# A hybrid decoder step on one core: other order of the last mixer iteration and of the first expert blocks

## What is computed

```python
h = rmsnorm(x) * (1 + sc_m) + sh_m
u = h @ w_in                      # conv_a | conv_b | q | k | v | g
y = concat[conv branch, retention branch] @ w_out
x = x + gt_m * y
h = rmsnorm(x) * (1 + sc_f) + sh_f
scores = sigmoid(h @ w_router)    # 64 experts: 4 of 8 groups kept, then 6 experts of a token
x = x + gt_f * (shared(h) + sum of the 6 experts' weight * expert(h))
y = rmsnorm(x, g_final)           # expert: (silu(h@w1) * (h@w3)) @ w2, hidden width 256
```

## Time and profile before

| | |
|---|---|
| median of 3 runs | 1592.87 us (1591.91 to 1594.37) |
| profiled execution, its time | 1594.62 us |
| its span in the profile | 1592.8 us |
| PE busy | 1439.1 us, 90% |
| DVE busy | 830.8 us, 52% |
| POOL busy | 493.3 us, 31% |
| HBM read, written | 323.10 MB, 62.13 MB |

### The profile page before, as it was taken

The page is one execution under the profiler, slowest core; times in us unless marked ns, Lnnn a source line. Parts: engine busy times, 40 slices in busy tenths (PEclk is TensorE's granted clock), DMA queues, the critical chain, the costliest instruction groups (busy, mean ns, idle before and its releaser), DMA issues.

```text
span 1592.8 us, 17516 instructions
## 1 busy us (share of the span) xinstructions
PE 1439.1 (90%) x5855; PEld 644.2 (40%) x5855; DVE 830.8 (52%) x2113; ACT 217.5 (14%) x369; POOL 493.3 (31%) x426
## 2 busy tenths in 40 slices
PE   4899999999999999998579999899999999999947
PEld 2344454555545454733233343233344333333313
DVE  1147778998988999733533332332333333323317
ACT  1111231312222131322000000000000000000003
POOL 0001010121211111311545454444545454545410
PEclk8899999999999999788789999999999999999978
DMA  9987211211120000512499999999999999999976
GB/s 333 328 317 262 95 43 66 82 40 70 40 82 27 32 29 28 192 39 78 145 331 320 371 367 373 366 362 370 367 372 367 371 370 348 340 373 366 367 211 244
DMA packets 93436, 369.69 MB, mean 232 GB/s; under 512 B 17741, under 2 KB 29425, under 8 KB 68207
## 3 DMA queue, kind: packets, MB, share of 16 engines
q1 hardware_dynamic: 69383, 304.29, 49.0%
q0 software_dynamic: 23968, 64.35, 16.3%
HBM read 323.10 MB, written 62.13 MB: 242 GB/s over the span
## 4 chain that ended last, share of the span: by engine, by line
DMA 44%; PE 25%; DVE 17%; issue 7%; SPq 4%; ACT 2%; POOL 1%; POOLq 0%; DVEq 0%; ACTq 0%
DMA acc_rows<-xr,kT 20%; DMA acc_rows<-W,kT 17%; PE U L649 9%; DVE cv L1249 7%; PE R L703 7%; DMA acc_rows<-W,shared_f 3%; PE U L851 2%; SPq L400 2%; DMA W<-in_w_ada 2%; PE U L828 1%; PE R L613 1%; PE U L805 1%; SPq L407 1%; DMA acc_rows<-xr,shared_f 1%; DMA x_t<-h_rows,q_r 1%
## 5 line engine op out<-in xcount | busy, mean ns | idle before, releaser
L649 PE MATMUL U<-W,hT 128*128 128x512 f32 x864 | 386.5, 602 | 1.2 <-issue 1.2
L1249 DVE SCALAR_TENSOR_TENSOR cv<-win,cw,cv 128x128 f32<-128x128 f32 x960 | 254.8, 343 | 1.4
L867 PE MATMUL R<-W,glu 128*32 128x512 f32 (+2 forms) x1024 | 240.9, 597 | 1.3 <-DVE glu L1537 1.3
L851 PE MATMUL U<-W,cat 128*128 128x512 f32 (+2 forms) x736 | 236.1, 608 | 5.5 <-issue 3.0
L649 PEld LDWEIGHTS U<-W,hT 128*128 128x128 f32 x864 | 162.9, 193 | 189.0 <-issue 189.0
L851 PE MATMUL U<-W,hT 128*32 128x512 f32 (+2 forms) x1312 | 237.2, 601 | 0.0
L1524 DVE STREAM_TRANSPOSE hT<-x_t 128x1024 f32<-128x1024 f32 x33 | 67.4, 2042 | 217.4 <-DMA x_t<-h_rows,q_r 215.6
L1524 DVE STREAM_TRANSPOSE cat<-W 128x1024 f32<-128x1024 f32 x33 | 67.2, 2037 | 214.2 <-DMA W<-h_rows,q_r 181.8
L867 PEld LDWEIGHTS R<-W,glu 128*32 128x32 f32 (+2 forms) x1024 | 84.1, 138 | 150.2 <-issue 148.8
L851 PEld LDWEIGHTS U<-W,cat 128*128 128x128 f32 (+2 forms) x736 | 93.2, 163 | 124.7 <-issue 121.1
L1718 POOL DMA_INDIRECT x_t<-h_rows,q_r x124 | 125.1, 1009 | 37.9 <-issue 37.9
(11 more groups left out here) (293 smaller groups left out, 1187.3 us busy)
## 6 DMA issues: line engine op xcount, KB each, us to landing
W<-in_w SPq DMA_DIRECT2D x192, 1024.0 KB, 17.5
W<-in_w_ada SPq DMA_DIRECT2D x24, 1024.0 KB, 9.3
W<-in_w_in SPq DMA_DIRECT2D x6, 2048.0 KB, 19.9
W<-acc_rows SPq DMA_DIRECT2D x16, 512.0 KB, 9.6
h_rows<-xr SPq DMA_DIRECT2D x9, 512.0 KB, 2.7
x_t<-in_x_prompt SPq DMA_DIRECT2D x8, 512.0 KB
W<-in_w_out SPq DMA_DIRECT2D x1, 4096.0 KB, 17.7
xr<-in_x_prompt SPq DMA_DIRECT2D x8, 512.0 KB
```

Source lines behind the costliest of these rows:

```text
L649: last = mm(U[BANK[g]][:, :], hT[:, k, :], w_in[:, k, 512 * g:512 * g + 512], start=k == 0, stop=k == KT - 1)
L851: last = mm(U[1][cols, :], xgT[z][:, k, cols], w13[:, :, k, :], start=k == 0, stop=k == KT - 1)
L867: last = mm(R[cols, 512 * half:512 * half + 512], hidT[:, f, cols], weights[:, at:at + 512], start=f == 0, stop=f == FT - 1)
L1249: ins = v.scalar_tensor_tensor(cv[:, c, :], win[:, c, w:w + P], cw[:, c, w:w + 1], cv[:, c, :], ALU.mult, ALU.add)
```

## The change

- `AHEAD` is 2 in place of 4: blocks 0 and 1 are shared, block 2 is the first routed unit, then shared and routed blocks take turns until block 15. The planner `even_order`, which uses AHEAD, gives another order of the groups on the line.
- The ring's slots are numbered in the order (0, 3, 1, 2), so that the first two don't lie on the samples' states; the samples' scaled k moves into `late`.
- SyncE: storing `new_ret_sample`, and waiting for it, moves from ahead of the first weight load to behind the loads of places 0 and 1.
- TensorE in the last mixer part: `mix_out(7)` is cut in halves with the samples' small sums and transposes between them; the samples' output product (`few_out`) is cut in parts, with `positions(6)`, the transposes of tile 7 and `router(7)` between them; state products 0 to 2 come after it, 3 and 4 after the first shared `up`, 5 to 7 around `rank_products`. The samples' router comes ahead of the first shared `up`. `positions(8)` follows that `up`; `spread_lists` comes ahead of block 1.
- DVE: `top_k(6)` goes ahead of `norm2(7)`, `place(6)` right behind it, `top_k(7)` is cut in two with `sample_residual` between; `place(7)`, `top_k(8)`, `place(8)` and the ranking follow with no block work among them. Blocks 1 and 2 come after the list's numbers and not between them.
- ACT: `score(7)` ahead of the state updates, which are spread among later steps.
- GpSimd: only gathers 0 and 1 come ahead of the lists; scatters 0 and 1 come after `slot_ready`, behind `gather(2)` and `gather(3)`.

```diff
-AHEAD = 4
+AHEAD = 2
-        ring = [W[:, WE * (r + 1):WE * (r + 2)] for r in range(RING)] + [shw]
+        ring = [W[:, WE * (r + 1):WE * (r + 2)] for r in (0, 3, 1, 2)] + [shw]
-        k_s = k_d[0:NS, :]
+        k_s = late[0:NS, 0, 1024:1536]
@@ SyncE
-            sp.wait_ge(state_upd, 2 * H)
-            for b in range(NS):
-                sp.dma_start(out["new_ret_sample"][0, b].rearrange("h d e -> d h e"),
-                             S0[:, b // 2, b % 2, :, :]).then_inc(newret_out, 16)
-            sp.wait_ge(newret_out, 16 * (NS + 1))
-            for s in range(NE):
+            for s in range(2):
+                load_in_line(s)
+            sp.wait_ge(state_upd, 2 * H)
+            for b in range(NS):
+                sp.dma_start(out["new_ret_sample"][0, b].rearrange("h d e -> d h e"),
+                             S0[:, b // 2, b % 2, :, :]).then_inc(newret_out, 16)
+            sp.wait_ge(newret_out, 16 * (NS + 1))
+            for s in range(2, NE):
                 load_in_line(s)
@@ TensorE
-            mix_out(TP - 1)
+            mix_half(TP - 1, 0)
             few_sum(sq, sum2_done)
             few_rows(o_t[:, :, :].rearrange("p h e -> p (h e)"), R24, ret_posed)
+            mix_half(TP - 1, 1).then_inc(wout_done, 1)
+            few_out(0, 0, KT)
+            positions(TP - 2, pick, NT)
             rows2_trans(TP - 1, hT_ready, NT)
-            state_product(0)
-            state_product(1)
-            router(TP - 1, TP)
-            state_product(2)
-            state_product(3)
-            positions(TP - 2, pick, NT)
-            up(0, shw_all, 0)
+            few_out(1, 0, KT // 2)
+            router(TP - 1, TP)
+            few_out(1, KT // 2, KT).then_inc(wout_done, 1)
+            for n in range(3):
+                state_product(n)
+            positions(TP - 1, pick, NT)
...
-            for n in range(H, 2 * H):
-                state_product(n)
...
-            hidden_trans(0)
-            up(1, shw_all, 1)
-            pe.wait_ge(state_upd, 2 * H)
-            positions(TP - 1, pick, NT)
-            down(0, shw_all)
-            positions(TP, pick_s[:, :], NT)
-            hidden_trans(1)
-            rank_products()
+            up(0, shw_all, 0)
+            positions(TP, pick_s[:, :], NT)
+            for n in range(3, 5):
+                state_product(n)
+            rank_products()
+            state_product(5)
+            hidden_trans(0)
+            for n in range(6, 2 * H):
+                state_product(n)
+            spread_lists()
-            for x in range(2, NX):
+            for x in range(1, NX):
                 await_weights(x)
                 up(x, parts_of(x), x % 2)
+                if x == 1:
+                    pe.wait_ge(state_upd, 2 * H)
                 down(x - 1, parts_of(x - 1))
                 hidden_trans(x)
-                if x == 2:
-                    spread_lists()
@@ VectorE
             residual(TP - 1)
+            top_k(TP - 2)
             norm2(TP - 1)
-            top_k(TP - 2)
+            place(TP - 2, pick, NT)
+            groups_kept(TP - 1)
             sample_residual()
-            place(TP - 2, pick, NT)
+            experts_kept(TP - 1)
             sample_norm2()
-            top_k(TP - 1)
-            blk_hid(0)
-            blk_hidT(0)
-            xpose(1)
             place(TP - 1, pick, NT)
...
-            block(1)
...
-            block(2)
+            blk_hid(0)
+            xpose(1)
+            blk_hidT(0)
...
+            block(1)
+            block(2)
             block(3)
@@ GpSimd
             ret_out(TP)
+            fill_list(TP - 2)
             gather(1)
-            fill_list(TP - 2)
             fill_list(TP - 1)
-            gather(2)
             fill_list(TP, NS)
-            gather(3)
...
-            scatter(0)
-            scatter(1)
             pool.wait_ge(slot_ready, 2)
-            gather(4)
-            for x in range(2, NX):
+            gather(2)
+            for x in range(NX):
                 if x + 3 < NX:
                     gather(x + 3)
                 scatter(x)
```

More of the change, by code:

```diff
@@ L696, in positions, with mix_half, mix_out @@
                 mm(cnt_m, mean_w[:, :], chosen, start=True, stop=True).then_inc(pos_done, 1)
-            def mix_out(m):
+            def mix_half(m, n):
                 pe.wait_ge(catA_part, 4 * (m + 1))
                 pe.wait_ge(catB_ready, m + 1)
-                for n in range(2):
-                    for k in range(KT):
-                        last = mm(R[:, 512 * n:512 * n + 512], cat[:, k, :], w_out[:, k, 512 * n:512 * n + 512],
-                                  start=k == 0, stop=k == KT - 1)
-                last.then_inc(wout_done, 1)
+                for k in range(KT):
+                    last = mm(R[:, 512 * n:512 * n + 512], cat[:, k, :], w_out[:, k, 512 * n:512 * n + 512],
+                              start=k == 0, stop=k == KT - 1)
+                return last
+            def mix_out(m):
+                mix_half(m, 0)
+                mix_half(m, 1).then_inc(wout_done, 1)
             def body(i, front=True, tail=True, route=True, nxt=True, place=True):
@@ L822, in _, with few_out @@
             few_rows(o_t[:, :, :].rearrange("p h e -> p (h e)"), R24, ret_posed)
+            mix_half(TP - 1, 1).then_inc(wout_done, 1)
+            def few_out(n, first, last):
+                for k in range(first, last):
+                    ins = mm(U[n][0:NS, :], cat_s[:, k, :], w_out[:, k, 512 * n:512 * n + 512], start=k == 0, stop=k == KT - 1)
+                return ins
             pe.wait_ge(catA_part, 4 * NT)
@@ L825, in _ @@
             pe.wait_ge(k_rot, NT)
-            for n in range(2):
-                for k in range(KT):
-                    last = mm(U[n][0:NS, :], cat_s[:, k, :], w_out[:, k, 512 * n:512 * n + 512], start=k == 0, stop=k == KT - 1)
-            last.then_inc(wout_done, 1)
+            few_out(0, 0, KT)
+            positions(TP - 2, pick, NT)
             pe.wait_ge(sret_ready, 1)
             rows2_trans(TP - 1, hT_ready, NT)
+            few_out(1, 0, KT // 2)
+            pe.wait_ge(dest_ready, TP - 1)
+            router(TP - 1, TP)
+            few_out(1, KT // 2, KT).then_inc(wout_done, 1)
             pe.wait_ge(vmask_ready, 1)
-            state_product(0)
-            state_product(1)
-            router(TP - 1, TP)
-            state_product(2)
-            state_product(3)
-            pe.wait_ge(score_ready, TP)
-            positions(TP - 2, pick, NT)
+            for n in range(3):
+                state_product(n)
             def tiles_of(parts):
@@ L1142, in _ @@
             nc.scalar.activation(std2[0:NS, :], ssq2[0:NS, :], ACT.Sqrt, scale=1.0 / D, bias=eps_c[0:NS, 0:1]).then_inc(norm2_std, 1)
+            state_update(1)
+            state_update(2)
             act.wait_ge(h2_posed, NT)
             nc.scalar.activation(h2T[:, :, 0:NS], Xk[:, :, 0:NS], ACT.Copy).then_inc(h2T_ready, 1)
-            for n in range(H, 2 * H):
-                state_update(n)
             act.wait_ge(ret_ready, NT)
@@ L1151, in _ @@
             blk_silu(0)
+            for n in range(3, 2 * H):
+                state_update(n)
             for x in range(1, NX):
@@ L1275, in top_k, with groups_kept @@
             def top_k(m):
+                groups_kept(m)
+                experts_kept(m)
+            def groups_kept(m):
                 dve.wait_ge(score_ready, m + 1)
```

14 lines of the change are left out of this document (7 added, 7 removed).

## The result

The changed kernel takes 1574.74 us (median of four runs, 1572.82 to 1576.92), the kernel before 1593.17 (four runs, 1591.91 to 1594.37) on the same chip: a ratio of 0.9885, interval [0.9868, 0.9902], 18.4 us less. The forecast was 1580 in a range of 1566 to 1590.

What follows compares the result with a forecast made beforehand. The prediction took the serial string of expert-stage scatters as the clock, with PE and DMA just behind. Start 17, step 3 and tail -7 gave 13 us off the 1592.87 median: 1580, range 1566 to 1590.

Steps and rivals of the forecast that it cites:

- start, at scatter 4: Start of the expert stage: earlier list numbers bring scatter 4 from 844.72 to 828, 17 us gained.
- step: Time between successive scatters in the expert stage: loads spread over 64 blocks instead of 62, 3 us gained in all.
- tail: Last blocks: up(64) waits for place 62's down part, 8 us and 2 for the clock, partly absorbed; 7 us lost.
- The numbers sooner: Reordered work on the list's numbers before the expert stage: line_ready at 743 instead of 779.88, some 37 us sooner.
- What is ahead of 692 us doesn't change: Work before tile 7's residual: the same 32 mix_out matmuls, cut by small ones, so times count from the same start.
- From `line_ready` to the first routed up: List writes, list gathers, spreading, then gather and transpose: from line_ready at 743 to the up at 780.
- The stores cost nothing: Moving 2 MB of state stores behind the first weight loads on SP's queue would cost no time; issuing takes 6 us.
- the cover of 20: Slack for weights of places 2 and 3: loaded until 780, wanted at 803, hiding the moved stores.
- the string is the clock of this stage: Expert stage: serial scatters, each waiting for the last to land, set the pace at 11.35 us a step.
- the 0.15: Sign of being wrong: the step between scatters moves by more than 0.15 us, which 64 blocks turn into 10 us.
- rival 1: Expert stage: bytes set the step, which gains 16 us; total gain 26 us, 1567 us; chance 0.18.
- the rule on queues: DMA engines take packets in turn from queues with work, so longer weight queues wouldn't lengthen scatters; step stays 11.35 us.

Runs made afterwards that it cites:

- late_place: Changed kernel, but the last token tile's numbers are again worked out behind shared block 0's up part; 1597.86 us, ratio 1.0028 to the kernel before.
- half: Changed kernel, but from place 4 on each expert's down-part load is cut to 64 KB, so results are wrong; 1543.07 us, ratio 0.9676 to the kernel before.
- split_tail2: Changed kernel with its last expert group moved to -3, place 0 loaded before the stores, place 1 after the lists land; 1567.95 us, ratio 0.9829 to before.
- hold: Changed kernel with the first weight load held back until both gathers of lists have landed; 1579.69 us, ratio 0.9921 to the kernel before.
- tables: Changed kernel, but odd blocks scatter to a second pair of tables, so no scatter waits for the one before; 1573.50 us, ratio 0.9864 to before.
- ahead4: Changed kernel with AHEAD back at 4, so blocks 0 to 3 are shared; 1577.21 us, ratio 0.9887 to the kernel before.
- early: Changed kernel with state products 3 to 6 ahead of positions(8), first shared up behind the ranking, stores before all loads; 1581.48 us, ratio 0.9929 to before.

## Why the prediction was right, and where it was not

The time came out 5.3 us below the forecast, inside the range and just under the forecast's own 1575 to 1585. Measured from the start of `mix_out(7)` (673.56 in the trace that the forecast counted on), term by term:

| term | forecast | measured |
|---|---|---|
| start, at scatter 4 | 17 | 12.6 |
| step | 3 | 8.4 |
| tail | -7 | -3.0 |
| sum | 13 | 18 |

Each of the three is 4 to 5 us off, one of them the other way. That the sum is only 5 off is in part luck: the start's 4.4 us too much covered most of the step's 5.4 too little.

- **The numbers sooner: right.** 743 was forecast and 740.9 is there; from `mix_out` that is 69.4 forecast and 70.8 measured (here the end of its row, as in the forecast). `late_place` shows that this moment carries the change. Two of its pieces went another way than told. Some of the products of the states came at the lower clock (the row at 742.55, where the granted clock is 0.50: 2.07 us for two matmuls that took 1.12 at 740.11, at 1.00), and so did a part of `few_out` (5.43 us for 8 matmuls at 700.98, 3.60 for 8 at 708.27). The first lay beside the path; the second, ahead of the router, took 1.3 us more than the 4.1 forecast; the granted clock from 700 to 706 is 0.61.
- **"What is ahead of 692 us doesn't change": not so.** PE's matmuls of `mix_out(7)` began 3.5 us sooner in this execution. As the medians don't show this as a gain, it belongs to the execution. It makes the absolute moments (778.60 for 780, 828.60 for 828) look sooner than they are: from `mix_out` scatter 4 was 4.1 us later than forecast, at 158.5 for 154.4, though `half`, with the same code up to there, was at 154.4.
- **From `line_ready` to the first routed up: right,** 37.9 us for 37; it was 35.6 to 37.1 in the others with this order, 33.8 in `split_tail2` with half the early weights, and 30.9 in `hold` with none beside the lists (all from the start of `line_ready`'s row). So the weights that are loaded early lengthen it by up to 7 us, and are needed all the same.
- **The stores cost nothing: right in the kernel as changed,** as places 2 and 3 went out at 767.32 and block 4 wasn't late. But they took 11.24 us to issue and not 6, and places 2 and 3 went out only behind them, 35.5 us ahead of block 4's `up` (802.80). In `hold` the same loads went out 23.0 us ahead of an `up` that waited for them. So by my estimate some 12 us of the cover of 20 were left.
- **The step: mis-sized, and half of its mechanism was missing.** What failed is "So the string is the clock of this stage", and with it "3 us, near the lower end". That the string holds the blocks is so (the waits ahead of L868), but it doesn't set the step by itself, as `tables` shows: the supply of weights stands at the same pace. Scatters land in 10.4 us in the median in both kernels, and still the step went from 11.46 to 11.31 us over blocks 4 to 60, just about the 0.15 that the prediction had set as a sign of being wrong. By the traces it went down because before has a block for which the weights came late (PE idles 3.05 us ahead of 1016.26, `ahead4` 5.49 ahead of 1000.11, both ahead of block 21, and the `up` that follows takes 9.12 and 8.68 us for 7.07), and the changed kernel has none up to block 60. In before this wait and the slow `up` make 5.1 of the 8.4 us; the rest isn't traced to a cause. So rival 1 had the right term, and its size was 8.4 us for 16; `half` shows that PE's own 10.79 us a block is as far as it could go. `ahead4` puts the whole of this term down to AHEAD, as the forecast did, and shows that AHEAD gives it back at the start (3.8) and in the tail (4.4).
- **The tail: right in place and kind,** a wait for place 62's down part ahead of block 64, issued 0.1 us behind the end of the `down` before it. 8 was forecast for the wait and 2 for the clock; it was 4.48 and 1.45 (8.54 us for an `up` of 7.09, its first 4.6 us at a granted clock of 0.68). The wait ended 4.87 us after the issue at 1478.53, sooner than any down part of before landed; the DMA engines had run empty just before. The rows show the DMA share and GB/s of 1470 to 1490 us, in 40 slices of 0.5; slices 16 to 19, from 1477.5 on, are all but idle:

```profile
DMA  9999999999999842001786998999999899999989
GB/s 408 431 400 401 426 344 311 205 180 205 213 229 234 299 173 80 35 0 33 131 262 246 442 459 360 442 410 393 393 410 328 262 352 246 311 328 295 369 238 344
```

Landing times in the changed kernel, line 488, line 492 and the scatters of line 1743:
```profile
DMA to landing us min/median/max: 7.9/13.9/25.5
```
```profile
DMA to landing us min/median/max: 6.8/17.3/20.1
```
```profile
DMA to landing us min/median/max: 5.9/10.4/12.0
```
The weights' up parts land 3.4 us sooner in the median than in before, the scatters just as before. This agrees with the rule on queues that the prediction quoted from the Trainium skill ("DMA: Bandwidth & Descriptors", section "Queues, rings and completion order"): a DMA engine takes packets in turn from the queues that have work, so a longer line on SP's queue need not lengthen a scatter on GpSimd's. In `half`, with 29% of the weights' bytes gone, the median of the scatters fell only to 9.5 us. The rule held, and the conclusion from it (the step stays) did not, since the scatters' landing alone doesn't set the step.

**Open.** That PE's idle lumps in `tables` are waits for weights is worked out from the order of the loads and their landing times, not shown by a releaser. Whether the supply of weights is limited by the DMA engines' rate or by the ring's depth was not separated: `half` eases both. And no experiment takes bytes away while it leaves the scatters' landing as it is.

## What to carry to other kernels

A chain of waits names one limit, and another may stand right behind it: when it shows one serial transfer after another with an equal step, look whether PE and DMA share are also full in that stretch, and take the wait away in an experiment before costing anything by it. Look also at where PE's idle time stands before and after: here its sum stayed and its cause changed. Where a kernel starts its main stage on a number that is worked out late, each microsecond of that number can be one of the time, as it was here; but what is let in beside it (weights ahead of the lists, stores behind the weights) has to be weighed in both directions, and here half of the early load did no worse than all of it, while none of it cost 8 us. Count moments of two traces from the first instruction that the change reorders, not from the start of the span.

## What the runs showed of the hardware

- Eight stores of 256 KB take SP 5.96 us to issue with no weights ahead of them, 6.15 behind the 3 MB of `split_tail2`, 11.24 behind the 6 MB of the changed kernel, and 19.61 right behind 6 MB in `hold`: issuing itself took longer the more was queued ahead. I had costed it at 6.
- Two matmuls of a state product took 1.12 us at 740.11 (granted clock 1.00) and 2.07 at 742.55 (0.50) in the same trace, with no gap on PE above 0.92 us (ahead of 739.38) since 724.90. In `early` the clock stayed at 0.50 from 726 to 740 us with PE busy throughout.
- `up(64)` went on 4.87 us after the issue of the 1 MB that it waited for. The least landing that the profile gives for this line in this kernel is 6.8 us; for the transfer of 1478.53 itself it gives none.
